# First pair of prompt tiles: when VectorE norms the second tile's rows, and which engine sums the weight blocks

## What is computed

```python
h = modulate(rmsnorm(x, g_mix), sh_a, sc_a)
u = jnp.dot(h, w_in)                       # (1024, 2208)
q_sb, k_sb, v_sb, q_lat, kv_lat, kpe_raw = jnp.split(u, SPLITS, axis=-1)
qm = jnp.dot(rmsnorm(q_lat, g_qa), w_qb)   # then norms and rotary
ckv_new = rmsnorm(kv_lat, g_kva)
kv = jnp.dot(ckv_all, w_kvb)
```

## Time and profile before

| | us |
|---|---|
| median of 3 runs | 1286.9 |
| lowest and highest of them | 1284.16, 1288.25 |
| the profiled execution | 1286.2 |
| its span, first to last instruction | 1284.6 |

### The profile page before, as it was taken

How to read it: one execution, slowest core, us unless ns; L and a number is a source line. 1 busy time by engine, 2 the same in 40 slices (tenths; PEclk the granted TensorE clock), 3 DMA queues, 4 the chain that set the end, 5 groups by cost and what they waited for, 6 DMA issues and landing times. The chain is left out here.

```text
span 1284.6 us, 18765 instructions
## 1 busy us (share of the span) xinstructions
PE 1169.2 (91%) x7144; PEld 656.3 (51%) x7145; DVE 716.8 (56%) x1382; ACT 351.2 (27%) x770; POOL 227.3 (18%) x254
## 2 busy tenths in 40 slices
PE   4799999999987997799999999899986899999996
PEld 1446556465543555566677767555553333343332
DVE  1546467374665885466777776545472343544444
ACT  1113122131322444156555545223331000000000
POOL 0200000000400003155433333001122112122111
PEclk9899999999998998889999999899986899999998
DMA  8803204132057889331111004262565999999993
GB/s 361 324 9 95 70 22 124 44 89 58 27 170 216 304 292 285 97 96 30 30 30 30 2 1 156 87 252 90 195 240 192 379 371 372 368 390 393 349 326 78
DMA packets 103275, 226.17 MB, mean 176 GB/s; under 512 B 21034, under 2 KB 61212, under 8 KB 87826
## 3 DMA queue, kind: packets, MB, share of 16 engines
q1 hardware_dynamic: 92562, 207.61, 45.0%
q0 software_dynamic: 7344, 17.33, 5.5%
q10 hardware_dynamic: 3280, 0.02, 0.1%
HBM read 192.37 MB, written 39.38 MB: 180 GB/s over the span
## 5 line engine op out<-in xcount | busy, mean ns | idle before, releaser
L2142 PE MATMUL f_C<-first_region,oT 128*128 128x512 f32 x256 | 115.1, 602 | 0.0
L2922 DVE TENSOR_TENSOR g_sig<-g_GU,g_sig 128x256 f32<-128x256 f32 x23 | 9.8, 425 | 156.4 <-ACT g_sig L2873 156.4
L2697 PE MATMUL g_GU<-late,first_region 128*32 128x512 f32 (+2 forms) x384 | 89.4, 620 | 4.6 <-issue 4.6
L1922 DVE TENSOR_TENSOR_SCAN region<-region,early 128x128 f32<-128x128 f32 (+7 forms) x64 | 88.5, 1403 | 5.0 <-POOL region L1726 4.9
L2697 PE MATMUL g_GU<-w_gu,first_region 128*32 128x512 f32 (+2 forms) x448 | 84.7, 594 | 3.8 <-issue 2.6
L2142 PEld LDWEIGHTS f_C<-first_region,oT 128*128 128x128 f32 x256 | 48.0, 193 | 54.2 <-issue 54.1
L2676 POOL DMA_INDIRECT y<-oT,g_li x22 | 34.9, 1586 | 217.6 <-DVE oT L2940 192.1
L1791 PE MATMUL e_Z<-first_region,region 104*128 104x512 f32 (+3 forms) x192 | 70.6, 505 | 0.2 <-ACT region L1884 0.2
L1734 POOL TENSOR_SCALAR region<-region,e_sm 128x128 f32<-128x128 f32 (+7 forms) x64 | 47.2, 748 | 130.2 <-DVE e_sm L1935 130.2
L1928 DVE TENSOR_REDUCE e_sm<-e_Z 128x1 f32<-128x128 f32 (+7 forms) x64 | 46.5, 747 | 23.0 <-PE e_Z L1791 22.1
L2873 ACT ACTIVATE g_sig<-g_GU 128x256 f32<-128x256 f32 x23 | 8.8, 384 | 181.4 <-PE g_GU L2697 181.4
(11 more groups left out here) (550 smaller groups left out, 2416.1 us busy)
## 6 DMA issues: line engine op xcount, KB each, us to landing
region<-w_ada SPq DMA_DIRECT2D x16, 1024.0 KB, 6.1
late<-w_gate SPq DMA_DIRECT2D x14, 1024.0 KB, 12.1
late<-w_up SPq DMA_DIRECT2D x14, 1024.0 KB, 18.6
late<-w_down SPq DMA_DIRECT2D x14, 1024.0 KB, 23.6
w_gu<-w_gate SPq DMA_DIRECT2D x12, 1024.0 KB, 12.1
w_gu<-w_up SPq DMA_DIRECT2D x12, 1024.0 KB, 18.7
w_down<-w_down SPq DMA_DIRECT2D x12, 1024.0 KB, 20.4
region<-w_in SPq DMA_DIRECT2D x3, 2048.0 KB, 16.9
```

Source lines behind the costliest of these rows:

```text
L1922: nc.vector.tensor_tensor_scan(back, back, least, 1.0, ALU.mult, ALU.max).then_inc(scan_done, 1)
L2142: end = nc.tensor.matmul(C[n % 2][:, c * 512:(c + 1) * 512], lhsT=g.oT[:, i, k, :], rhs=wo[:, k, c * 512:(c + 1) * 512], start=k == 0, sto ...
L2697: end = nc.tensor.matmul(GU[h * n:h * n + n, :], lhsT=xT[:, b, k, h * n:h * n + n], rhs=wgu[s][:, :, k, :], start=k == 0, stop=k == KD - 1 ...
```

## The change

Three edits in `phase_b`. POOL's four instructions for `sums[2]` and `sums[3]` go, with POOL's waits; DVE executes the same four instructions in a new function `other_weights_summed`, called behind `rows_summed(0)` and ahead of the first `combine`. `weights_summed` is renamed. And `xn_of(1)` moves from behind the latent norms of tile 0 to directly behind `hT_of(0)`, ahead of `body(0)`.

```diff
         @block.gpsimd
         def _(pool):
-            in_lat, in_v, in_q, in_k = g.w_in_loaded
             step = Steps(pool, pool_step)
-            pool.wait_ge(in_k, 16)
-            for k in range(0, HALF, 2):
-                end = nc.gpsimd.tensor_tensor(sums[2][k // 2].rearrange("p (s n) -> p s n", s=2),
-                                              g.w_in[:, HALF + k:HALF + k + 2, SBW:2 * SBW],
-                                              g.w_in[:, k:k + 2, SBW:2 * SBW], ALU.subtract)
-            end.then_inc(t_late, 1)
-            pool.wait_ge(in_q, 16)
-            pool.wait_ge(t_early, 2)
-            for k in range(0, HALF, 2):
-                end = nc.gpsimd.tensor_tensor(sums[3][k // 2].rearrange("p (s n) -> p s n", s=2),
-                                              g.w_in[:, HALF + k:HALF + k + 2, 0:SBW],
-                                              sums[1][k // 2].rearrange("p (s n) -> p s n", s=2), ALU.subtract)
-            end.then_inc(t_late, 1)
             pool.wait_ge(prod_mm, PROD * PT // 2)
...
-            def weights_summed():
+            def other_weights_summed():
+                for k in range(0, HALF, 2):
+                    end = nc.vector.tensor_tensor(sums[2][k // 2].rearrange("p (s n) -> p s n", s=2),
+                                                  g.w_in[:, HALF + k:HALF + k + 2, SBW:2 * SBW],
+                                                  g.w_in[:, k:k + 2, SBW:2 * SBW], ALU.subtract)
+                end.then_inc(t_late, 1)
+                dve.wait_ge(t_early, 2)
+                for k in range(0, HALF, 2):
+                    end = nc.vector.tensor_tensor(sums[3][k // 2].rearrange("p (s n) -> p s n", s=2),
+                                                  g.w_in[:, HALF + k:HALF + k + 2, 0:SBW],
+                                                  sums[1][k // 2].rearrange("p (s n) -> p s n", s=2), ALU.subtract)
+                end.then_inc(t_late, 1)
+
+            def first_weights_summed():
...
                 else:
-                    if first:
-                        xn_of(1)
                     hT_of(i + 1)
                     if first:
-                        weights_summed()
+                        first_weights_summed()
                     else:
                         back(i - 1, 1)
                     rows_summed(i)
+                    if first:
+                        other_weights_summed()
                     combine(i, U2_AT)
...
             hT_of(0)
+            xn_of(1)
             tiles(body)
```

## The result

| | before | after |
|---|---|---|
| median of 4 runs each, us | 1287.38 | 1277.63 |
| lowest and highest | 1284.16, 1288.25 | 1276.08, 1278.38 |
| the profiled execution | 1286.2 | 1278.38 |
| its span | 1284.6 | 1276.8 |

The ratio is 0.9927, with a 95% interval of 0.9908 to 0.9947: 7 to 12 us faster. (This ratio, like those further down, is taken over all runs of both kernels; it is not the quotient of the two medians.) The median fell by 9.7 us, the span of the profiled executions by 7.8.

What follows compares the result with a forecast made beforehand. PE, busy 91%, was held by product 2's start, which waited for DVE's row sums, blocked by POOL. Terms of 2.05, 4.31 and 2.41 us sum to 8.77, taken as 8.7: median 1278.2 us, range 1274.8 to 1282.4.

Steps and rivals of the forecast that it cites:

- Product 2 at 58.5 to 58.6: First pair on PE: DVE's sums, chained from the k columns' landing, let product 2 start there instead of at 67.32.
- PE early enough: PE ahead of product 2: product 1 ends at 56.4 to 56.5, leaving PE idle for about 2.1 us.
- The four added instructions at nothing: On DVE behind L896: 4.7 us of added sums, done by 63.9, cost nothing; L905 runs 4.9 us ahead of need.
- become the bound (3%): Rival, 3%: all eight weight sums on DVE delay product 5 above 2.9 us each (d); at 3.27, 3.1 us slower.
- DMA as the cause of the long L876 (2%): Rival, 2%: DMA traffic, not POOL, made DVE's L876 long; product 2 starts at 62.8, gaining only 4.5 us.
- this other reading: L876 runs at half rate beside POOL instead of blocked: 2.3 us expected, against 3.27 in the trace.
- the first rival: The rival, 2%, that DMA made L876 long, not POOL: 4.5 us gained, 1282.4.
- The early load of tile 2's rows at nothing: SP's queue: the load moves from 51.70 to about 49.6, delaying the k columns 0 to 1.3 us; taken as 0.
- Later than 52: Sign that the forecast is wrong: the k columns land later than 52; 51.85 was assumed for DVE.
- The gain is lost later (6%): Rival, 6%: in later stages, around an expert's weight wait, 5 us or more could go: 1283 to 1287.
- The clock at the new wait (8%, 3.4 us): Rival, 8%: PE's clock falls to half at the remaining wait ahead of product 2, costing 3.4 us: 1281.6.
- The three terms: DVE's path to product 2: unblocked L876 2.05 us, unblocked L892 and L894 4.31, earlier L876 start 2.41; sum 8.77.

Runs made afterwards that it cites:

- the two repetitions: The changed kernel run again without edit, beside the kernel before: medians 1278.66 us against 1285.57, and 1276.51 against 1285.47.
- The threefold version: Against the changed kernel, DVE makes the four added weight sums three times over, writing the same values: median 1284.14 us, 1285.77 for the kernel before beside it.

## Why the prediction was right, and where it was not

**Product 2 at 58.5 to 58.6.** It started at 58.62. The chain from the landing of the k columns held link by link: 51.91 for 51.85, 2.36 for each pair of weight sums, 0.6 from one row sum to the next, 58.46 for the end of L893, 0.16 us to PE.

**PE early enough.** Transposes from 44.75, v columns in 7.03 at full clock, end of product 1 at 56.09 for my 56.4; the wait was 2.53 for 2.1, because PE's transposes began 0.35 us earlier than I had put them (44.75 for 45.1) while the k columns landed at the same time. In the two repetitions the wait was 2.14 and 2.11.

**The four added instructions at nothing.** 2.35 us for each two, ended at 63.73, L904 never late. So DVE did not become the bound (3%): the d of that rival came out at 1.18 us, and it needed 2.4. The threefold version shows the edge where I had put it.

**DMA as the cause of the long L876 (2%).** Excluded: L875 ran at 51.91 under the same full DMA traffic (a share of 1.02 from 51.9 to 54.3, and 1.04 before) in 2.36 us for the two. That POOL and DVE would each run at half rate is excluded too, by the 3.36 and 3.41 us of L876's instructions with `xn_of(1)` alone early, since half rate would make them 2.36. My sentence that this other reading would lead to the first rival doesn't follow: half rate beside POOL also ends when POOL is silent, and gives the same 8.7; only the DMA reading leads there.

**The early load of tile 2's rows at nothing.** It moved to 49.27, and the k columns released DVE at 51.91, against 51.81 for POOL before. In the two repetitions it was 52.10 and in the experiments with that early load 51.86 to 52.28, and there is only one such time without it, so a delay of some tenths of a us is not excluded. "Later than 52" was one of my signs of being wrong; it came true in the repetitions, and product 2 started only 0.2 us later (58.81 and 58.80).

**The gain is lost later (6%).** It was not. The late load of an expert's weights starts at 1177.05 instead of 1183.73 and ends 7.6 us earlier: it moved with the work ahead of it.

**The clock at the new wait (8%, 3.4 us).** Here the prediction was too sure and the size wrong: the rival to which I gave 8% came true. The fall came in all three profiles of the changed kernel, behind waits of 2.53, 2.14 and 2.11 us, and cost 1.8 us each time, half of what I had priced: I took a stretch at half clock of 6.8 us from the earlier trace rows, and it was 3.4 us long. What I took as evidence against it, the old wait of 3.25 us without a fall, was one execution. Waits of 2.89 and 2.69 us in two experiments had no fall either, so the length of the wait alone doesn't decide. What does is open.

**The three terms.** Their sum, 8.77, is right for both halves together. As worths of the parts (6.36 for POOL's silence, 2.41 for the early start) they are wrong, and the wording invited that reading: alone, the early start is worth 0 and the silence 3 to 4. I had noted that a gain ahead of product 1 is lost unless L894 moves, and that the k columns' landing starts POOL, but not that POOL would then simply take the time that an earlier L876 wins.

**The total.** 1277.63 for 1278.2. The mechanism was right, but so close an agreement is luck. The 8.7 us contained no fall of the clock. In the profiled execution 8.7 us at product 2 became 7.0 at product 3, 7.3 where the prompt's attention starts and 7.8 at the end, while the median moved 9.7, and 6.9 and 9.0 in the repetitions. Of these differences I can say only that they are within what runs of one kernel differ by. The profiled execution was the slowest of its four runs; whether the clock also fell in the other three, no record tells.

## What to carry to other kernels

Before work is moved off an engine, look at what else that engine's timing does: here POOL's help was not too slow, it ran at the moment when it blocked the critical VectorE sums, and one wait was as good as the move. Two engines that block each other and start on the same landing share the time behind it, however early one of them is made ready, so price the halves of a change separately before adding their terms. And after a stall is shortened, fill the rest from the stalled engine's own list: exchanging two independent products was worth another 2 to 4 us, up to 1.8 of them the clock.

## What the runs showed of the hardware

- A GpSimd tensor_tensor from SBUF and a VectorE tensor_tensor with both inputs in SBUF take turns, one whole instruction each: 6.69 us in place of 2.36 for two VectorE sums (3.36 and 3.41) beside two of POOL's (2.35 and 3.33). GpSimd memsets beside them cost nothing (2.36), nor did POOL's sums hold a VectorE instruction with one operand in PSUM (0.69).
- The same GpSimd sums took 4.66 us for two when nothing blocked them, 5.63 when they took turns with VectorE; VectorE took 2.36.
- TensorE's granted clock fell to half behind waits of 2.11, 2.14 and 2.53 us in the midst of dense 512-column products (product 2 in 5.37 us for 3.60), and not behind 1.60, 1.86, 2.69, 2.89 and 3.25 us at the same place, nor behind 0.69 us ahead of product 3. It also fell behind a wait of 4.85 us and within one of 10.27 us. I had expected the shorter ones to be harmless.
